# A mixture-of-experts decoder step: longer weight runs in ten slots, rows gathered two experts ahead

## Chip, cores, metric

The kernel runs on one core of a Trainium2 chip, with no other core at work. The metric is the device time of one execution in microseconds (us). "Span" is the time from the first to the last instruction in the profile of one execution.

## The reference, cut to what matters

One layer of a decoder runs on 280 tokens (16 meta tokens, 256 prompt tokens, 8 sample tokens) of width 2048, all in float32. An input projection feeds two recurrent branches, an output projection and a residual add give `x1`, and then comes the part that the change is about:

```python
xs = rmsnorm(x1, norm_ffn)                   # 280 x 2048
grp = top-1 of 4 expert groups               # softmax of xs @ w_coarse + b_coarse
e0, e1 = top-2 of the 8 experts in grp       # softmax of xs @ w_fine + b_fine
for e in 32 experts:                         # only the rows routed to e count
    act = silu(xs @ w_gate[e]) * (xs @ w_up[e]) * gate[:, e]   # 2048 x 512 each
    out += act @ w_down[e]                                      # 512 x 2048
y = rmsnorm(x1 + out, norm_final)
```

Each expert has 3 x 2048 x 512 float32 weights, 12.58 MB; the 32 experts have 403 MB, and all of it is read once.

## The kernel before, in words

**Stages.** After loads and norms come the input projection with the S5 scan, the HGRN2 heads, the output projection (L1174 to L1195, 8 blocks of 2.1 MB of `w_out` through ring slots 0 to 3), routing (L1198 to L1213 and L1650 to L1734), then the expert loop (`round_loads`, `round_act`, `round_rows`, `round_pe`, `round_dve`, one per engine, 32 experts in 16 double steps, b = 0 and 1), and a tail that adds each token's two expert rows to `x1`, normalises and stores. Every engine's stream is written out by hand and ordered by semaphores. A second round of the expert loop exists for experts with over 64 rows.

**Weights.** The ring has six slots of 2.1 MB: slots 2, 3, 0, 1 for an expert's gate and up weights, first half of the 2048 input rows and then the second, and 4, 5 for the two halves of its down weights. SyncE issues the loads in that order (L384, L390); gate and up of expert x+1 wait until TensorE has used that half of expert x, and down likewise. So the ring holds one expert. A load's rows are dealt `(k p) n`: partition p gets row k*128 + p for each k, in runs of one row: 2 KB for gate and up (8 runs a partition), 8 KB for down (2 runs).

**Rows.** `x1` goes to a DRAM tensor `x1_dram` (L499). For each expert VectorE makes a one-hot placing (L1740), TensorE turns it into a list of up to 64 tokens in bank 7 (`list_of`, L1221), VectorE reads indices and scales out of it (L1745 to L1750), and GpSimd gathers the 64 rows by an indirect DMA (L822) into one of two buffers, on partitions 0 to 63. TensorE transposes them in 16 steps (`turn_64`, L1228), with the rows as the stationary operand, 128 adjacent columns each; VectorE scales them by `norm_ffn` on the way out (L1755). The rows of expert x+1 are listed and gathered while TensorE is in gate and up of expert x.

**An expert on TensorE (L1244 to L1285).** List for x+1, 64 matmuls for gate and up (L1261), 16 transposes of the next rows, a wait for SiLU (L726), up (L727) and their product (L1780), 4 transposes of the product, a copy (L1785), and 32 matmuls with the down weights (L1282). ScalarE copies the result out (L732), GpSimd scatters it into `y_dram` (L839), waits for that to land and only then comes to its next gather.

Of the kernel before, what the change touches and what calls it, by code (L numbers as in the profile page):

```python
# [32 lines left out]
ALU = mybir.AluOpType  # L33
# [31 lines left out]
def hymba_step(nc, t):  # L65
# [27 lines left out]
    with ctx:  # L93
# [15 lines left out]
        vecs = sb("vecs", [P, 80])  # L109
        sc5 = sb("sc5", [P, 6, NJ])  # L110
# [104 lines left out]
        oh = Carver(arena, xnT_at)(3, CAP)  # L215
        c = Carver(arena, tab_at)
        lgT = Carver(arena, tab_at)(T)
        _, xg0, xg1 = c(D), c(D), c(D)
        xg = [xg0, xg1]
        yout = [c(D), c(D)]  # L220
        assert c.at <= AR_N
        c = Carver(arena, 0)
# [9 lines left out]
        gfin = Carver(arena, xnT_at + 3 * CAP)(D)  # L232
        ynorm = Carver(arena, tab_at)(D)
        V_COLS = D - 640

        route = sb("route", [P, 707])
# [5 lines left out]
        rankm = c(3, NE + 1)  # L242
        PL = c(3, NE + 1, 4)
        maxn, ext, mvals = c(1), c(ROUNDS - 1), c(33)
        assert c.at <= 707
# [4 lines left out]
        idx_dst = [sb(f"idx_dst{i}", [CAP, 1], U32) for i in range(2)]  # L250
        gcol = [sb(f"gcol{i}", [CAP, 1]) for i in range(2)]
# [12 lines left out]
        def sems(names):  # L264
# [3 lines left out]
        vec_loaded, s5_loaded, bc_loaded, wr_loaded = sems("vec_loaded s5_loaded bc_loaded wr_loaded")  # L268
        slot_loaded = [sem(f"slot_loaded{i}") for i in range(6)]
# [33 lines left out]
            "moe_done gfin_loaded ysum_done f_rms out_ready out_stored")  # L303
        yrow_loaded = [sem(f"yrow_loaded{i}") for i in range(3)]
# [16 lines left out]
        FILLS = [len(range(s, NPRE, PRE_SLOTS)) for s in range(4)] + [0, 0]  # L321
        MOE_SLOT = (2, 3, 0, 1)
# [36 lines left out]
        def slot(s, k):  # L359
            return ring[:, s, :].rearrange("p (k n) -> p k n", k=k)  # L360

        def run_rounds(eng, one_round):

            one_round(0)
            eng.wait_ge(lists_ready, 1)
            extra = eng.value_load(extra_i[0:1, 0:1], min_val=0, max_val=ROUNDS - 1)
            with eng.If(extra > 0):
                with eng.Fori(0, extra) as r:
                    one_round(r + 1)

# [8 lines left out]
        def _(sp):  # L379
            def load_gate_up(e, q):  # L380
                w = t["w_gate"] if q % 2 == 0 else t["w_up"]
                half = D // 2
                src = w[0][bass.ds(e, 1), (q // 2) * half:(q // 2 + 1) * half, :]
                sp.dma_start(slot(MOE_SLOT[q], KD // 2), src.rearrange("a (k p) n -> p (a k) n", p=P)) \  # L384
                    .then_inc(slot_loaded[MOE_SLOT[q]], 16)

            def load_down(e, s):
                half = FH // 2
                src = t["w_down"][0][bass.ds(e, 1), (s - 4) * half:(s - 3) * half, :]
                sp.dma_start(slot(s, KF // 2), src.rearrange("a (k p) n -> p (a k) n", p=P)) \  # L390
                    .then_inc(slot_loaded[s], 16)
# [24 lines left out]
            def load_vectors():  # L416
                for name, at in (("norm_mix", V_MIX), ("norm_ffn", V_FFN), ("s5_D", V_D), ("s5_b_glu", V_BGLU),
                                 ("s5_out_gain", V_G5), ("hg_lb_logits", V_LB0), ("hg_out_gain", V_GH)):
                    rows = t[name].rearrange("a (k p) -> (a k) p", p=P)
                    sp.dma_start(vrow[at:at + rows.shape[0], :], rows).then_inc(vec_loaded, 16)  # L420

# [53 lines left out]
            for n in range(OUT_AT + 2, NPRE):  # L475
                pre_load(n)
            for b in range(2):
                sp.wait_ge(S0_stored[b], 16 * len(range(b, NS, 3)))
# [6 lines left out]
            def round_loads(R):  # L485
                with sp.Fori(1 if is_first(R) else 0, NE) as e:
                    x = e + R * NE
                    for q in range(4):

                        sp.wait_ge(gate_up_done, x * 2 + (q // 2 - 1))  # L490
                        load_gate_up(e, q)
                    for s in (4, 5):
                        sp.wait_ge(down_done, x * 2 + (s - 5))
                        load_down(e, s)
# [6 lines left out]
            sp.wait_ge(logit_done, 1)  # L501
            sp.dma_start(gfin, t["norm_final"].rearrange("(a n) -> a n", a=1).broadcast_to([P, D])).then_inc(gfin_loaded, 16)

            run_rounds(sp, round_loads)
# [8 lines left out]
            for i, tile in enumerate(TILE_ORDER):  # L513
# [3 lines left out]
                if tile == 0:  # L517
                    sp.dma_start(y[0:P - NM, :], x1[NM:P, 0, :]).then_inc(out_stored, 16)
                elif tile == 1:
                    sp.dma_start(y[P - NM:2 * P - NM, :], x1[:, 1, :]).then_inc(out_stored, 16)  # L520
                else:
                    sp.dma_start(y[2 * P - NM:SEQ, :], x1[0:LAST, 2, :]).then_inc(out_stored, 16)
                    sp.dma_start(t["y_sample"][:, 0, :], x1[LAST:LAST + NS, 2, :]).then_inc(out_stored, 16)
# [9 lines left out]
        def _(act):  # L533
# [162 lines left out]
            act.wait_ge(S0_stored[2], 16 * len(range(2, NS, 3)))  # L696
            for o in range(NO):
                step.settle()
                for tile in range(3):
                    n = TT[tile]  # L700
                    act.wait_ge(x1_ready, 2 * o + 1 + tile // 2)
                    ins = nc.scalar.activation(yout[0][0:n, tile * CB:(tile + 1) * CB], x1[0:n, tile, o * CB:(o + 1) * CB], ACT.Square,
# [15 lines left out]
            def round_act(R):  # L718
                with act.Fori(0, NE // 2) as i:
                    for b in range(2):  # L720
# [10 lines left out]
                        for cc in range(4):  # L731
                            ins = nc.scalar.activation(yout[b][0:CAP, cc * 512:(cc + 1) * 512],  # L732
# [4 lines left out]
            for i, tile in enumerate(TILE_ORDER):  # L737
# [4 lines left out]
                step.link(nc.scalar.activation(ynorm[0:n, :], x1[0:n, tile, :], ACT.Square, accum_out=s))  # L742
# [5 lines left out]
        def _(pool):  # L748
# [67 lines left out]
            def gather(g, p):  # L816
# [5 lines left out]
                pool.indirect_dma_start(out=xg[p][0:CAP, :], out_offset=None, in_=x1_dram,  # L822
# [3 lines left out]
            def round_rows(R):  # L826
                if not is_first(R):
                    pool.wait_ge(tr_done, R * (NE + 1) + 1)
                gather(R * (NE + 1), 0)
                with pool.Fori(0, NE // 2) as i:  # L830
                    for b in range(2):
                        x = i * 2 + (R * NE + b)
                        g = i * 2 + (R * (NE + 1) + b + 1)

                        pool.wait_ge(tr_done, g)
                        gather(g, 1 - b)
# [3 lines left out]
                                                in_=yout[b][0:CAP, :], in_offset=None, bounds_check=last_row,  # L840
                                                oob_is_err=False).then_inc(scattered[b], 16)
                        pool.wait_ge(scattered[b], i * 16 + (R * (NE // 2) + 1) * 16)
                        pool.sem_inc(rows_free, 1)

# [5 lines left out]
            def add_rows(tile):  # L850
                n = TT[tile]
                pool.wait_ge(yrow_loaded[tile], 32)
                xt = x1[0:n, tile, cols]
# [3 lines left out]
            def norm_rows(i, tile):  # L857
# [3 lines left out]
                xt = x1[0:n, tile, cols]  # L861
# [15 lines left out]
        def _(pe):  # L877
# [347 lines left out]
            def turn_64(out, rows, waits):  # L1225

                eye = ident[0:CAP, 0:CAP]
                return pe.matmul(out, rows, eye, start=True, stop=True) if waits else pe.transpose(out, rows, eye)  # L1228

            def transpose_rows(p):  # L1230
                for k in range(KD):
                    ins = turn_64(PB[4 + k // 8][:, (k % 8) * CAP:(k % 8 + 1) * CAP], xg[p][0:CAP, k * P:(k + 1) * P], k == 0)
                ins.then_inc(tr_done, 1)

            def round_pe(R):
# [3 lines left out]
                else:  # L1239
                    pe.wait_ge(dst_ready, R * (NE + 1))  # L1240
                    pe.wait_ge(xgT_ready, R * (NE + 1))
                list_of(R * (NE + 1), 0)
                pe.wait_ge(gathered[0], R * (16 * 17) + 16)
                transpose_rows(0)  # L1244
                with pe.Fori(0, NE // 2) as i:
                    for b in range(2):
# [3 lines left out]
                        pe.wait_ge(dst_ready, g)  # L1250
                        list_of(g, i * 2 + (b + 1))

                        pe.wait_ge(xgT_ready, g)
                        for half in range(2):
                            sg_, su_ = MOE_SLOT[2 * half], MOE_SLOT[2 * half + 1]
                            pe.wait_ge(slot_loaded[sg_], x * 16 + 16 * (FILLS[sg_] + 1))
                            pe.wait_ge(slot_loaded[su_], x * 16 + 16 * (FILLS[su_] + 1))
# [591 lines left out]
```

## Time and profile before

| | |
|---|---|
| median of 3 runs | 1838.98 us (1836.88 to 1843.45) |
| the profiled execution | 1840.96 us, span 1838.9 us |
| granted TensorE clock, mean | 0.912 |
| bytes moved by DMA | 505.27 MB |
| output projection | 548 to 690 us |
| routing | 690 to 716 us |
| expert loop | 716 to 1790 us |
| tail | 1790 to 1839 us |

Loop and tail start and end where TensorE's first gate matmul starts and its last down matmul ends. DMA rates in GB/s are of the 16 queue engines together. A "share" of the DMA over 1 means that packets overlap on an engine.

### The profile page before, as it was taken

What the parts mean: (1) busy time and instruction counts of PE and PEld (TensorE: products, weight loads), DVE (VectorE), ACT (ScalarE), POOL (GpSimd) and SP (SyncE); (2) the same over time, 40 slices, a digit from 0 to 9 for tenths busy, and PEclk for the clock granted to TensorE, in tenths of its full rate; (3) what the DMA queues carried; (4) which work ended last, traced back from release to release, by engine and by line L of the source; (5) the groups of instructions that cost most, each with busy time, mean ns of one, the idle gap of its engine ahead of it and who ended that gap; (6) DMA issues with size and microseconds to landing.
All of it is one profiled execution on the core that took longest, in us unless ns stands there. A gap on an engine that the chain in (4) does not pass through costs nothing.

```text
span 1838.9 us, 19426 instructions
## 1 busy us (share of the span) xinstructions
PE 1486.7 (81%) x7565; PEld 839.3 (46%) x7565; DVE 566.0 (31%) x1407; ACT 285.2 (16%) x565; POOL 296.1 (16%) x402
## 2 busy tenths in 40 slices
PE   6899999798989996878787788788787787777870
PEld 5677776577758773433233233233233232233330
DVE  2779999666651223101010010010010010010015
ACT  2111111333320001111111011011011011011111
POOL 0066665333200000000000000000000000000006
PEclk9899999999979997988988998888999998899895
DMA  9324242335317625999999999999999999999964
GB/s 284 117 92 138 92 138 92 116 118 163 108 29 230 229 92 193 395 398 393 378 382 369 377 384 387 381 376 372 383 370 373 380 378 376 372 387 390 367 241 151
DMA packets 253055, 505.27 MB, mean 275 GB/s; under 512 B 23572, under 2 KB 99556, under 8 KB 233708
## 3 DMA queue, kind: packets, MB, share of 16 engines
q1 hardware_dynamic: 235788, 493.74, 74.5%
q0 software_dynamic: 5200, 9.19, 1.6%
q10 hardware_dynamic: 12016, 1.66, 0.6%
q8 instruction: 32, 0.52, 0.1%
q14 instruction: 19, 0.16, 0.0%
HBM read 503.18 MB, written 26.28 MB: 288 GB/s over the span
## 4 chain that ended last, share of the span: by engine, by line
DMA 35%; PE 26%; SPq 6%; DVE 1%; POOL 1%; issue 1%; ACT 0%; POOLq 0%; ACTq 0%; DVEq 0%
DMA ring<-in_w_up_dram 34%; PE bank L1261 16%; SPq L384 6%; PE bank L1191 6%; PE bank L1282 1%; PE bank L900 1%; DMA ring<-expert_rows 0%; PE bank L1158 0%; PE bank L1141 0%; POOL arena L862 0%; POOL arena L863 0%; PE bank L1169 0%; DVE arena L1798 0%; PE bank L1211 0%; PE bank L1228 0%
## 5 line engine op out<-in xcount | busy, mean ns | idle before, releaser
L1261 PE MATMUL bank<-ring,arena 128*64 128x512 f32 x2048 | 518.8, 664 | 156.8 <-DMA ring<-in_w_up_dram 156.8
L1261 PEld LDWEIGHTS bank<-ring,arena 128*64 128x64 f32 x2048 | 196.4, 152 | 452.6 <-issue 452.6
L1282 PE MATMUL bank<-ring,arena 128*64 128x512 f32 x1024 | 259.8, 666 | 19.0 <-DVE arena L1785 19.0
L1780 DVE SCALAR_TENSOR_TENSOR arena<-arena,gcol 64x512 f32<-64x512 f32 x32 | 23.8, 743 | 728.8 <-ACT arena L727 728.8
L930 PE MATMUL bank<-arena,ring 128*128 128x280 f32 x768 | 188.8, 405 | 3.0 <-ACT arena L579 1.9
L930 PEld LDWEIGHTS bank<-arena,ring 128*128 128x128 f32 x768 | 145.9, 192 | 44.1 <-issue 7.6
L1282 PEld LDWEIGHTS bank<-ring,arena 128*64 128x64 f32 x1024 | 80.5, 152 | 174.6 <-issue 174.6
L839 POOL DMA_INDIRECT expert_rows<-arena,idx_dst x32 | 29.5, 922 | 800.2 <-ACT arena L732 800.2
L732 ACT ACTIVATE arena<-bank 64x512 f32<-64x512 f32 x128 | 75.9, 593 | 330.0 <-PE bank L1282 328.8
L1191 PE MATMUL bank<-ring,arena 128*128 128x256 f32 x512 | 114.8, 386 | 0.0
L1228 PE MATMUL bank<-ident,arena 64*128 64x64 f32 x721 | 66.3, 239 | 56.7 <-DVE arena L1780 47.5
L1191 PEld LDWEIGHTS bank<-ring,arena 128*128 128x128 f32 x512 | 98.2, 193 | 17.1 <-issue 3.7
L822 POOL DMA_INDIRECT arena<-x_rows,idx_tok x33 | 31.0, 939 | 447.1 <-DVE gcol L1747 229.4
L1228 PEld LDWEIGHTS bank<-ident,arena 64*128 64x128 f32 x721 | 57.3, 155 | 87.2 <-DVE arena L1780 51.8
L1011 PE MATMUL bank<-arena,ring 128*128 128x280 f32 x256 | 74.4, 417 | 0.0
L1745 DVE TENSOR_SCALAR idx_tok<-bank 64x1 uint32<-64x1 f32 x33 | 5.0, 150 | 223.5 <-PE bank L1221 223.5
L726 ACT ACT_TABLE_LOAD x16 | 20.5, 1283 | 337.1 <-PE bank L1261 337.1
L726 ACT ACTIVATE arena<-bank,rcol 64x512 f32<-64x512 f32 x32 | 21.8, 683 | 289.6 <-PE bank L1261 289.4
L1495 DVE TENSOR_TENSOR_SCAN arena<-sc,arena 128x272 f32<-128x272 f32 x64 | 60.4, 983 | 1.1
L922 PE MATMUL bank<-ring,arena 128*128 128x256 f32 x256 | 59.5, 390 | 0.0
L922 PEld LDWEIGHTS bank<-ring,arena 128*128 128x128 f32 x256 | 49.1, 195 | 10.2 <-issue 3.6
L782 POOL TENSOR_TENSOR arena<-arena 128x272 f32<-128x272 f32 x32 | 21.8, 682 | 173.8 <-PE bank L987 91.3
(333 smaller groups left out, 1403.9 us busy)
## 6 DMA issues: line engine op xcount, KB each, us to landing
ring<-in_w_down_dram SPq DMA_DIRECT2D x64, 2048.0 KB, 21.2
ring<-in_w_gate_dram SPq DMA_DIRECT2D x64, 2048.0 KB, 19.6
ring<-in_w_up_dram SPq DMA_DIRECT2D x64, 2048.0 KB, 22.6
ring<-in_w_in_dram SPq DMA_DIRECT2D x20, 2048.0 KB, 8.7
ring<-in_w_out_dram SPq DMA_DIRECT2D x8, 2048.0 KB, 9.7
ring<-in_s_w_glu_dram SPq DMA_DIRECT2D x2, 2048.0 KB, 8.4
arena<-v_samples SPq DMA_DIRECT2D x8, 512.0 KB, 4.4
ring<-expert_rows SPq DMA_DIRECT2D x4, 1024.0 KB, 9.3
```

The source lines that it names most:

```text
L384: sp.dma_start(slot(MOE_SLOT[q], KD // 2), src.rearrange("a (k p) n -> p (a k) n", p=P)) \
L726: nc.scalar.activation(sg[0:CAP, :], PB[b][0:CAP, :], ACT.Silu, scale=rcol[b][:, 0:1])
L732: ins = nc.scalar.activation(yout[b][0:CAP, cc * 512:(cc + 1) * 512], PB[2 + cc // 2][(cc % 2) * CAP:(cc % 2 + 1) * CAP, :], ACT.Copy)
L822: pool.indirect_dma_start(out=xg[p][0:CAP, :], out_offset=None, in_=x1_dram, in_offset=bass.IndirectOffsetOnAxis(ap=idx_tok[p][:, 0:1], ax ...
L922: ins = pe.matmul(bank[:, tile * CB:(tile + 1) * CB], xnT[:, k, tile * P:(tile + 1) * P], w[:, k, :], start=(k == 0), stop=(k == KD - 1))
L930: ins = pe.matmul(bank[:, 0:T], w[:, k, b * P:(b + 1) * P], xnT[:, k, :], start=(k == 0), stop=(k == KD - 1))
L1011: ins = pe.matmul(PB[2][:, 0:T], slot(s, KD)[:, k, (i % 2) * P:(i % 2 + 1) * P], xnT[:, k, :], start=(k == 0), stop=(k == KD - 1))
L1191: ins = pe.matmul(PB[unit % 4][:, tile * CB:(tile + 1) * CB], yT[k][:, tile * P:(tile + 1) * P], slot(s, KD)[:, k, :], start=(k == 0), sto ...
L1228: return pe.matmul(out, rows, eye, start=True, stop=True) if waits else pe.transpose(out, rows, eye)
L1261: ins = pe.matmul(PB[b][at:at + CAP, :], xgT[b][:, kk, :], slot(s, KD // 2)[:, k, :], start=(kk == 0), stop=(kk == KD - 1))
L1282: ins = pe.matmul(PB[2 + cc // 2][at:at + CAP, :], hT[:, f, :], slot(4 + half, KF // 2)[:, k, cc * 512:(cc + 1) * 512], start=(f == 0), st ...
L1495: step.add(nc.vector.tensor_tensor_scan(M2[:, z], sc5[:, 0, j:j + 1].broadcast_to([P, TP]), M1[:, z], 0.0, ALU.mult, ALU.add))
```

## The change

Weights: all expert loads are dealt `(p k) n`, so that a partition gets one piece of DRAM of 16 KB (8 rows of gate or up, 2 rows of down). To match, the transposes take columns 8 apart (rows) and 2 apart (product), and a copy of `norm_ffn` in that order is loaded. There are ten slots: the six of the ring, two where the tables of the scan were, and two over `x1` itself. Gate and up have two sets of four slots, one for even and one for odd experts; down has ring slots 2 and 3. `x1` is read back from DRAM into two of the slots at the end. Rows: the list and the gather of expert x+2 are made in expert x; the two row buffers, and the two output buffers, are now the lower and upper 64 partitions of one tensor each. Some scratch moves (ScalarE's squares go to bank 7).

```diff
+        c = Carver(arena, x1_at)
+        x1_slots = [c(SLOT), c(SLOT)]
+        oh = c(3, CAP)
+        yout_both = c(D)
...
         c = Carver(arena, tab_at)
+        tab_slots = [c(SLOT), c(SLOT)]
+        xg_both = c(D)
...
+        x1_end, gfin = c(3, D), c(D)
...
+        halves = [slice(0, CAP), slice(CAP, P)]
+        xg, yout = ([buf[rows, :] for rows in halves] for buf in (xg_both, yout_both))
...
-        MOE_SLOT = (2, 3, 0, 1)
+        slots = [ring[:, i, :] for i in range(6)] + tab_slots + x1_slots
+        GATE_UP = ((6, 7, 4, 5), (0, 1, 8, 9))
+        DOWN = (2, 3)
...
-                sp.dma_start(slot(MOE_SLOT[q], KD // 2), src.rearrange("a (k p) n -> p (a k) n", p=P)) \
+                sp.dma_start(slot(s, KD // 2), src.rearrange("a (p k) n -> p (a k) n", p=P)) \
...
-            for n in range(OUT_AT + 2, NPRE):
+            for n in range(OUT_AT + 2, OUT_AT + 4):
                 pre_load(n)
+            sp.wait_ge(os_done, NS)
...
-            for s in (4, 5):
-                load_down(0, s)
             for q in range(4):
-                sp.wait_ge(out_done, 2 * (NO - 3 + q))
-                load_gate_up(0, q)
+                load_gate_up(0, 0, q)
+            for n in range(OUT_AT + 4, NPRE):
+                pre_load(n)
+            for h in range(2):
+                sp.wait_ge(out_done, 2 * (NO - 3 + h))
+                load_down(0, h)
+            sp.wait_ge(out_done, 2 * (NO - 1))
+            load_gate_up(1, 1, 0)
             sp.wait_ge(x1_ready, 2 * NO)
             for tile in range(3):
                 sp.dma_start(x1_dram[tile * P:tile * P + TT[tile], :], x1[0:TT[tile], tile, :]).then_inc(x1_stored, 16)
+            load_gate_up(1, 1, 1)
+            sp.wait_ge(x1_stored, 48)
             sp.wait_ge(logit_done, 1)
+            for q in (2, 3):
+                load_gate_up(1, 1, q)
+            def round_loads(R):
+                def down(x, e):
+                    for h in range(2):
+                        sp.wait_ge(down_done, x * 2 + (h - 1))
+                        load_down(e, h)
+                if is_first(R):
+                    down(1, 1)
+                with sp.Fori(1 if is_first(R) else 0, NE // 2) as i:
+                    for b in range(2):
+                        x = i * 2 + (R * NE + b)
+                        for q in range(4):
+                            sp.wait_ge(gate_up_done, x * 2 + (q // 2 - 3))
+                            load_gate_up(i * 2 + b, b, q)
+                        down(x, i * 2 + b)
...
+            sp.wait_ge(gate_up_done, extra * (2 * NE) + (2 * NE - 2))
+            for tile in TILE_ORDER:
+                sp.dma_start(x1_end[0:TT[tile], tile, :], x1_dram[tile * P:tile * P + TT[tile], :]).then_inc(x1_back[tile], 16)
...
-                        pool.wait_ge(tr_done, g)
-                        gather(g, 1 - b)
+                        pool.wait_ge(tr_done, i * 2 + (R * (NE + 1) + b + 2))
+                        gather(i * 2 + (R * (NE + AHEAD) + b + AHEAD), b)
                         pool.wait_ge(rows_ready, x + 2)
...
-                    ins = turn_64(PB[4 + k // 8][:, (k % 8) * CAP:(k % 8 + 1) * CAP], xg[p][0:CAP, k * P:(k + 1) * P], k == 0)
+                    half, kk = divmod(k, KD // 2)
+                    rows = xg[p][:, half * (D // 2):(half + 1) * (D // 2)].rearrange("t (p k) -> t k p", k=KD // 2)[:, kk, :]
+                    ins = turn_64(PB[4 + half][:, kk * CAP:(kk + 1) * CAP], rows, k == 0, p)
...
                         dve.wait_ge(act_ready, x + 1)
                         STT(hh[0:CAP, :], sg[0:CAP, :], gcol[b][:, 0:1], up[0:CAP, :], ALU.mult, ALU.mult).then_inc(h_made, 1)
+                        dve.wait_ge(h_made, x + 2)
+                        indices(g + 1, b)
                         dve.wait_ge(rows_free, x + 2)
-                        destinations(1 - b)
+                        destinations(g, 1 - b)
```

## Rows read from the trace of the kernel before

**Rows 1.** The page: the large DMA queue, and the chain by engine

```profile
q1 hardware_dynamic: 235788, 493.74, 74.5%
...
DMA 35%; PE 26%; SPq 6%; DVE 1%; POOL 1%; issue 1%; ACT 0%; POOLq 0%; ACTq 0%; DVEq 0%
```

**Rows 2.** Busy by stretch: length, engines, clock, DMA share, GB/s

```profile
780.00:1760.00 980.00, 764.34 (x3570) 308.56 (x3570) 86.38 (x261) 123.39 (x187) 52.91 (x57) 0.90 1.03 380
...
724.00:745.00 21.00, 18.15 (x91) 8.01 (x88) 2.70 (x6) 2.56 (x3) 0.00 (x0) 0.92 0.93 331
...
705.00:712.00 7.00, 1.54 (x11) 1.48 (x12) 1.12 (x8) 0.00 (x0) 1.12 (x1) 0.50 0.01 2
```

**Rows 3.** Chain of waits in the expert loop: start, us, what

```profile
759.60 3.04 SPq L384
...
960.25 3.47 SPq L384
963.82 20.28 DMA ring<-in_w_up_dram
...
984.24 9.69 PE bank L1261 x32
994.08 4.62 SPq L384
```

**Rows 4.** DMA packets of two stretches: 928 to 935 us, 949 to 953 us

```profile
DMA packets 1341, 2.71 MB, mean 387 GB/s; under 512 B 17, under 2 KB 17, under 8 KB 1341
...
DMA packets 232, 1.73 MB, mean 432 GB/s; under 512 B 10, under 2 KB 10, under 8 KB 25
```

**Rows 5.** Three whole stretches of down loads, by stretch as in rows 2

```profile
978.00:987.00 9.00, 4.81 (x18) 1.54 (x16) 0.00 (x0) 0.00 (x0) 0.93 (x1) 0.76 1.03 411
1013.00:1022.00 9.00, 4.64 (x20) 1.62 (x18) 0.00 (x0) 0.00 (x0) 0.94 (x1) 0.90 1.02 423
1047.00:1058.00 11.00, 6.08 (x22) 2.02 (x20) 0.00 (x0) 0.00 (x0) 0.93 (x1) 0.84 1.02 392
```

**Rows 6.** Timeline of TensorE over one expert: start, us, instructions, [idle before]

```profile
993.85 1.37 PE L1228 MATMUL bank<-ident,arena 64*128 64x64 f32 x17
997.43 0.62 PE L1228 MATMUL bank<-ident,arena 64*128 64x64 f32 x5 [2.21 <-DVE arena L1780]
998.64 8.78 PE L1282 MATMUL bank<-ring,arena 128*64 128x512 f32 x32 [0.59 <-DVE arena L1785]
1007.25 0.46 PE L1221 MATMUL bank<-route,arena 128*64 x6
1008.30 7.09 PE L1261 MATMUL bank<-ring,arena 128*64 128x512 f32 x32 [0.59 <-DMA ring<-in_w_up_dram]
1019.74 8.78 PE L1261 MATMUL bank<-ring,arena 128*64 128x512 f32 x32 [4.36 <-DMA ring<-in_w_up_dram]
```

**Rows 7.** SyncE's queue about the start of the loop

```profile
688.39 0.37 SPq L384 DMA_DIRECT2D ring<-in_w_up_dram  x1
690.19 1.35 SPq L499 DMA_DIRECT2D x_rows<-arena  x3
...
725.12 0.40 SPq L384 DMA_DIRECT2D ring<-in_w_gate_dram  x1
...
741.95 3.81 SPq L390 DMA_DIRECT2D ring<-in_w_down_dram  x2
```

**Rows 8.** Chain of waits, first and last expert

```profile
708.01 3.18 DMA arena<-x_rows,idx_tok
...
715.96 15.86 PE bank L1261 x63
...
1783.26 7.11 PE bank L1282 x32
```

**Rows 9.** The tile x_rows: who waited for the gathers; landing

```profile
  PEld bank L1228: 14.3, 7
...
DMA to landing us min/median/max: 3.2/7.5/9.0
```

**Rows 10.** Line L1228, 780 to 1760 us: duration in ns, min/median/max

```profile
L1228 PEld LDWEIGHTS bank<-ident,arena x638: 137/140/333, 791.8 to 1749.6; 64*128 64x128 f32 x160
```

More of the change, by code:

```diff
@@ L250, in hymba_step @@
         idx_dst = [sb(f"idx_dst{i}", [CAP, 1], U32) for i in range(2)]
+        dcol = [sb(f"dcol{i}", [CAP, 1]) for i in range(2)]
         gcol = [sb(f"gcol{i}", [CAP, 1]) for i in range(2)]
@@ L267, in hymba_step @@
         x_loaded = [sem(f"x_loaded{i}") for i in range(3)]
-        vec_loaded, s5_loaded, bc_loaded, wr_loaded = sems("vec_loaded s5_loaded bc_loaded wr_loaded")
-        slot_loaded = [sem(f"slot_loaded{i}") for i in range(6)]
+        vec_loaded, s5_loaded, bc_loaded, wr_loaded, gain_loaded = sems("vec_loaded s5_loaded bc_loaded wr_loaded gain_loaded")
+        slot_loaded = [sem(f"slot_loaded{i}") for i in range(10)]
         pool_consts, dve_consts, act_step, dve_step, pool_step = sems("pool_consts dve_consts act_step dve_step pool_step")
@@ L303, in hymba_step @@
             "moe_done gfin_loaded ysum_done f_rms out_ready out_stored")
+        x1_back = [sem(f"x1_back{i}") for i in range(3)]
         yrow_loaded = [sem(f"yrow_loaded{i}") for i in range(3)]
@@ L319, in hymba_step @@
         NPRE = OUT_AT + NO
-        FILLS = [len(range(s, NPRE, PRE_SLOTS)) for s in range(4)] + [0, 0]
-        MOE_SLOT = (2, 3, 0, 1)
+        FILLS = [len(range(s, NPRE, PRE_SLOTS)) for s in range(4)] + [0] * 6
+        slots = [ring[:, i, :] for i in range(6)] + tab_slots + x1_slots
+        GATE_UP = ((6, 7, 4, 5), (0, 1, 8, 9))
+        DOWN = (2, 3)
         EIGHTHS = 8
@@ L359, in slot @@
         def slot(s, k):
-            return ring[:, s, :].rearrange("p (k n) -> p k n", k=k)
+            return slots[s].rearrange("p (k n) -> p k n", k=k)
         def run_rounds(eng, one_round):
@@ L420, in load_vectors @@
                     sp.dma_start(vrow[at:at + rows.shape[0], :], rows).then_inc(vec_loaded, 16)
+                sp.dma_start(ffn_gain[:, :, :], t["norm_ffn"][0].rearrange("(h p k) -> p h k", h=2, p=P)).then_inc(gain_loaded, 16)
             for tile in TILE_ORDER:
@@ L474, in _ @@
             sp.dma_start(wr[:, :, NG:NG + NE], t["w_fine"][0].rearrange("(k p) n -> p k n", p=P)).then_inc(wr_loaded, 16)
-            for n in range(OUT_AT + 2, NPRE):
+            for n in range(OUT_AT + 2, OUT_AT + 4):
                 pre_load(n)
+            sp.wait_ge(os_done, NS)
+            for b in range(3):
+                sp.wait_ge(S0_stored[b], 16 * len(range(b, NS, 3)))
             for b in range(2):
-                sp.wait_ge(S0_stored[b], 16 * len(range(b, NS, 3)))
-            for s in (4, 5):
-                load_down(0, s)
+                sp.wait_ge(st_stored[b], 16 * NH // 2)
             for q in range(4):
-                sp.wait_ge(out_done, 2 * (NO - 3 + q))
-                load_gate_up(0, q)
[L485 to L494, printed above, removed]
+                load_gate_up(0, 0, q)
[6 more added lines that the diff above has]
+            load_gate_up(1, 1, 0)
             sp.wait_ge(x1_ready, 2 * NO)
@@ L828, in round_rows @@
                     pool.wait_ge(tr_done, R * (NE + 1) + 1)
-                gather(R * (NE + 1), 0)
+                for p in range(AHEAD):
+                    gather(R * (NE + AHEAD) + p, p)
                 with pool.Fori(0, NE // 2) as i:
@@ L843, in round_rows @@
                         pool.sem_inc(rows_free, 1)
+                pool.wait_ge(gathered[1], R * (16 * 17) + 16 * 17)
             run_rounds(pool, round_rows)
@@ L1223, in list_of, with turn_64 @@
                 ins.then_inc(list_done, 1)
-            def turn_64(out, rows, waits):
-                eye = ident[0:CAP, 0:CAP]
+            def turn_64(out, rows, waits, half):
+                eye = ident[halves[half], halves[half]]
                 return pe.matmul(out, rows, eye, start=True, stop=True) if waits else pe.transpose(out, rows, eye)
@@ L1654, in _ @@
             dve.wait_ge(part_logits, 1)
-            dve.wait_ge(S0_stored[2], 16 * len(range(2, NS, 3)))
             step.link(nc.vector.tensor_copy(lgT[0:NL, :], PB[6][0:NL, 0:T]))
@@ L1767, in round_dve @@
                     dve.wait_ge(rows_free, R * NE + 2)
-                places(0)
-                indices(g0, 0)
-                destinations(0)
-                rows_in(g0, 0)
+                for p in range(AHEAD):
+                    if p or not is_first(R):
+                        dve.wait_ge(list_done, g0 + p)
+                    places(p)
+                    indices(g0 + p, p)
+                destinations(g0, 0)
+                rows_in(t0, 0)
                 with dve.Fori(0, NE // 2) as i:
```

118 lines of the change are left out of this document (66 added, 52 removed).

## The prediction

> **What bounds the kernel now.** I read the page first: one DMA queue moves 493.74 of 505.27 MB and the chain that ends last is 35% DMA [rows 1], so the loads of weights are where to look. Then the busy times by stretch: in the expert loop, 780 to 1760 us, the DMA share is 1.03 at 380 GB/s, while TensorE is busy for 764 of 980 us at a mean granted clock of 0.90, that is, part of the time at the lower of its two levels, 1.2 GHz [rows 2]. A full DMA does not yet say that its rate sets the time, so I read the chain of waits: it repeats one figure, a half of gate and up on TensorE, SyncE's issue, a load of up weights of 20 us, the next half [rows 3]. From 759.60 to 994.08 us there are seven such turns, **33.5 us an expert**. The 20 us are mostly queueing: at 384 GB/s they are 7.8 MB, of which the load itself has 2.1. Bytes agree: 12.58 MB of weights, and some 0.3 MB of gathered and scattered rows, in 33.5 us are 384 GB/s. So the loop is bound by the DMA's rate, and freeing slots earlier would not by itself make it shorter.
>
> Could the rate rise? The DMA table for two short stretches shows that it depends on the run. In 928 to 935 us only the 2 KB packets of gate and up run, 387 GB/s; in 949 to 953 us nearly all bytes are the 8 KB packets of down, 432 GB/s [rows 4].
>
> **Weights in long runs.** Undisturbed, an expert now takes 8.39 MB / 387 + 4.19 MB / 432 = 21.7 + 9.7 = 31.4 us; measured are 33.5, so 2.1 us go to interruptions, row traffic among them. With 16 KB runs no row shows the rate; the nearest is the 8 KB one. Undisturbed: 12.58 / 432 = 29.1 us, the lower bound. Whole stretches of down loads with the row traffic in them run at 411, 423 and 392 GB/s [rows 5], by length 407; all weights at that rate take 30.9 us, and the 0.3 MB of rows 0.7 more: 31.7 us, the upper bound, since it has the row traffic hit all the time as it hits the down stretch. I take **31.2**, nearer to the upper end because the row traffic stays. That is 2.3 us an expert less.
>
> A rule speaks against this. The Trainium skill, DMA: Bandwidth & Descriptors, Specifications, gives 512 B as the least transfer for line rate; by it, 2 KB runs would be at line rate and longer ones would bring nothing. Here 387 against 432 GB/s [rows 4] disagrees. By the rule the sum would be that of the second rival.
>
> **Slots and order at the start.** Now the ring holds expert 0 at the start and expert 1's first load goes out at 725.12, when half of expert 0 has been used [rows 7]; between 705 and 712 us the DMA is idle (share 0.01) [rows 2]. After: gate and up of expert 0 go out during the output projection. They queue ahead of the third pair of `w_out` blocks: 8.4 MB, some 22 us, against blocks that are used 17.5 us apart and loaded four ahead, so TensorE does not feel it. Then down 0, and the first gate load of expert 1 before `x1` is stored at 690.19 [rows 7]; the other three behind it. These 8.6 MB (2.3 of rows, 6.3 of weights) run from 690 to about 712 us, so the first gather, at 708, no longer meets an idle DMA. Its 3.2 us [rows 8] become at most the median under load, 7.5 [rows 9]: between 0 and 4.3 us later, I take 3, as the queue is nearly drained. The second gather, the list of expert 1 and its indices run during the first gather: nothing; without that cover about 2 us once.
>
> SyncE then stands at down 1, which waits for the first half of down 0, now at 741.95 [rows 7], so at 745; behind that wait everything is queued, gate and up of expert 2 too, whose slots are free: the DMA idles from about 712 to 745. So the 8.4 MB of new room bring little: the old kernel has loaded 21 x 331 = 7.0 MB for expert 1 by then [rows 2]. From there the queue never runs dry: gate and up of x go out when x-2 is done, and down of x when down of x-1 is: 7 us after that was loaded, while gate and up of x still load for 14. The end of loading is 745 + 10.4 (down 1) + 30 x 31.2 = **1691 us**. Gate and up of expert 31 are there 10.4 us earlier, 1681; its second half takes 8.78, product and transposes 4.79 (993.85 to 998.64) [rows 6], down 7.11 [rows 8]: 1702. In the old kernel the last down ends at 1783.26 + 7.11 = 1790.4 [rows 8]. Gain **88.7 us**.
>
> **TensorE as the next in line.** Its own work in an expert, without waits for weights, is 7.09 + 8.78 (gate, up) + 13.9 (from 993.85 to 1008.30, less 0.59 of waiting) = 29.8 us [rows 6], under 31.2. That is the cover for all that follows.
> - Transposes from strided columns: not in the trace. The 17 instructions take 1.37 us and TensorE then waits 2.21 [rows 6], so they may become 2.6 times as long at no cost; a stationary load takes 140 ns now [rows 10]. Lower bound no change; upper below.
> - VectorE: a fourth index operation and a copy of the destinations (0.15 us each at most) between product and hT, beside 0.62 us of transposes: 0, or 0.1 us an expert without cover.
> - Gathers two ahead: TensorE waited 14.3 us in all for them [rows 9], while the DMA went on. 0 now, as the DMA sets the end; up to 14 if TensorE did.
> - GpSimd: the gather of x+2 waits for indices made after the product of x, before its scatter has data. Nothing stands behind it that is late.
> - ScalarE's squares in PSUM with one more wait, the second copy of `norm_ffn`: off the path.
> - `x1` read back and the last gain, 3.3 MB, behind the last down load: 8 us, until 1699, before the tail wants them at about 1717. Cover: the last down and the scatter; without it 8 us.
>
> The tail is otherwise the same. Sum: span 1838.9 - 88.7 = 1750.2. The profiled execution has 2.1 us around its span and stands 2.0 over the median of the runs, so the prediction for a run is **1750 us**.
>
> **Rivals.**
> 1. *Disturbances go with the short packets.* Then 29.1 us an expert, and TensorE's 29.8 decide: 719 + 32 x 29.8 = 1673, time 1721. For: the down stretches dip less. Against: the row traffic is unchanged. 9%.
> 2. *Long runs buy nothing* (they are still cut at each row, or DRAM gives no more). 33.5 us stay, only the start gains: 745 + 11.2 + 30 x 33.5 = 1761, end of down 1771, time 1819. For: no row has a 16 KB packet. Against: the 432 GB/s [rows 4]. 10%.
> 3. *TensorE becomes the bound through the transposes.* At twice their length: 17 x 0.28 - 3.58 = 1.2 and 4 x 0.14 = 0.6 more, 31.6 us an expert, 719 + 32 x 31.6 = 1730, time 1779. 9%. The Trainium skill, SBUF — State Buffer, Specifications (TRN2), asks for two hits in each 16-byte line for full bandwidth; columns 8 apart have one. No row shows such a load; doubling would be this rival.
> 4. *Slower: the same loads three times as long.* 420 ns each: 17 x 0.42 - 3.58 = 3.6 and 4 x 0.28 = 1.1, 34.5 us an expert, 719 + 32 x 34.5 = 1823, time 1872. It decides from 33.5 us on (1790 = 719 + 32 x 33.5), that is from about 370 ns a transpose. Against: the moving side, 64 columns, is unchanged, and 2.2 us are free. 4%.
>
> **How the numbers follow.** The forecast has 68%. Its bounds, 29.1 to 31.7 us an expert and 0 to 4.3 at the start, give 1721 (where TensorE stops it) to 1766. The range takes in rivals 1 and 3 and leaves out 2 and 4: 1705 to 1790, the low end below 1721 because TensorE at its higher clock all through would need less than 29.8. Faster by over 0.3% (5.5 us, about what a measurement can tell): the forecast and rivals 1 to 3, 96%, less one for what was not foreseen, 0.95; slower 0.03 and the same 0.02 share rival 4, whose price passes through zero near 370 ns, and the unforeseen.
>
> **What would show it.** Right: packets of over 8 KB in place of the 2 KB ones, about 410 GB/s in the loop, 31 us from expert to expert, the chain still of loads, the transposes within 3.6 us, TensorE waiting a little for weights, an idle DMA at about 715 to 745. Wrong: 380 GB/s with long packets; or a DMA share well under 1 in the loop with TensorE busy throughout; or transposes that end after the product is made.

## The result, and the profile after

The changed kernel takes **1774.04 us** (median of 4 runs, 1771.44 to 1777.56) where the kernel before takes 1839.9 us beside it: a ratio of 0.9645, 95% interval 0.9632 to 0.9658. The forecast was 1750 us, the range 1705 to 1790; 66 us are gained, 89 were forecast. The profiled execution takes 1773.67 us with a span of 1771.7.

The page of the changed kernel: the large queue (packets, MB, share), the queue of gathers and scatters, the chain by engine.

```profile
q1 hardware_dynamic: 113504, 496.04, 71.8%
q0 software_dynamic: 5280, 9.19, 1.6%
...
DMA 32%; PE 29%; issue 2%; DVE 2%; POOL 2%; SPq 1%; ACT 1%; POOLq 0%; ACTq 0%; DVEq 0%
```

Nearly the same bytes go in half as many packets as in [rows 1]. DMA and TensorE now share the chain almost evenly.

In the changed kernel L1310 is gate and up, L1333 down, L1271 the transposes; L401 issues the loads of gate and up, L407 those of down. In other runs these numbers shift by some lines. PE is TensorE's matmuls, PEld its loads of stationary operands, SPq SyncE's queue.

Busy by stretch, columns as in [rows 2]: start and end, length, busy us of PE, PEld, VectorE, ScalarE and GpSimd (with instructions), TensorE's clock, DMA share, GB/s.

```profile
705.00:712.00 7.00, 4.34 (x21) 4.24 (x22) 4.85 (x29) 0.00 (x0) 0.00 (x0) 0.50 1.01 425
712.00:745.00 33.00, 22.85 (x120) 12.46 (x119) 4.23 (x21) 2.56 (x3) 2.24 (x3) 0.76 0.18 73
780.00:1690.00 910.00, 774.92 (x3566) 340.15 (x3563) 86.69 (x288) 124.97 (x189) 53.08 (x58) 0.91 1.00 409
...
934.00:956.00 22.00, 20.95 (x104) 10.18 (x103) 3.04 (x10) 3.65 (x6) 1.86 (x2) 0.93 1.01 428
956.00:962.00 6.00, 5.53 (x30) 2.10 (x26) 0.00 (x0) 0.70 (x2) 0.00 (x0) 0.96 1.02 300
1056.00:1062.00 6.00, 6.00 (x24) 1.79 (x22) 0.00 (x0) 0.00 (x0) 0.00 (x0) 0.76 0.71 213
```

The DMA, idle before between 705 and 712 us, is full there, and idle from 712 to 745 instead. In the loop it moves 409 GB/s, 380 before [rows 2]. Two kinds of dip pull the mean under the 428 of an undisturbed stretch: at 956 the share stays at 1.02 while the rate falls to 300 (the rows of the gather issued at 952.21 pass), and at 1056 the share itself falls to 0.71 (nothing is queued).

DMA packets from 946 to 955 us, where hardly any rows move:

```profile
DMA packets 268, 3.90 MB, mean 433 GB/s; under 512 B 30, under 2 KB 30, under 8 KB 30
```

Packets of 16 KB thus run at 433 GB/s, as the 8 KB ones of [rows 4] did at 432.

The chain of waits (start, us, what), to be held against [rows 3, 8].

```profile
713.74 6.03 DMA arena<-x_rows,idx_tok
...
724.75 15.41 PE bank L1310 x63
...
810.43 37.14 DMA ring<-in_w_up_dram
...
998.48 40.98 DMA ring<-in_w_up_dram
1039.60 9.89 PE bank L1310 x32
...
1054.62 9.22 PE bank L1333 x32
...
1066.23 37.03 DMA ring<-in_w_up_dram
...
1636.68 39.54 DMA ring<-in_w_up_dram
1676.36 8.80 PE bank L1310 x32
1690.04 8.78 PE bank L1333 x32
1699.05 13.84 PE bank L1310 x64
...
1716.53 7.11 PE bank L1333 x32
```

The first three experts are TensorE's alone (no load in the chain until 810.43), and in the fourth it waits 0.35 us for one. Then a load of up weights of some 40 us, a half of gate and up, a down, and the next load repeat every second expert. From 810.43 to 1636.68 there are 26 experts: **31.8 us an expert**, 33.5 before. The last 47 us are TensorE's again.

SyncE's queue, as in [rows 7]:

```profile
750.34 3.76 SPq L407 DMA_DIRECT2D ring<-in_w_down_dram  x2
...
1060.43 3.77 SPq L407 DMA_DIRECT2D ring<-in_w_down_dram  x2
1064.74 0.33 SPq L401 DMA_DIRECT2D arena<-in_w_gate_dram  x1
```

Both dips of the share end with a down load: SyncE had stood waiting for the down slot, with the gate load queued behind it.

TensorE's timeline (as [rows 6]), and line L1271 (as [rows 10]):

```profile
982.43 2.33 PE L1271 MATMUL bank<-ident,arena 64*128 64x64 f32 x17
986.01 0.78 PE L1271 MATMUL bank<-ident,arena 64*128 64x64 f32 x5 [1.26 <-DVE arena L1837]
```

```profile
L1271 PEld LDWEIGHTS bank<-ident,arena x638: 189/203/353, 794.2 to 1689.1; 64*128 64x128 f32 x160
```

A stationary load of strided columns takes 203 ns (140 before). The 17 transposes grow from 1.37 to 2.33 us, and TensorE still waits 1.26 us for the product.

### The profile page after: what moved, and what is told of

It reads as the page before. It is cut to its first block, busy times and chain, and to the rows that moved or that the text cites. A ratio compares the mean times of both kernels' runs of the same rounds, so it can differ in the third digit from the quotient of the medians.

```text
span 1771.7 us, 19520 instructions
## 1 busy us (share of the span) xinstructions
PE 1504.0 (85%) x7571; PEld 873.4 (49%) x7571; DVE 566.3 (32%) x1445; ACT 285.1 (16%) x565; POOL 297.8 (17%) x403
## 3 DMA queue, kind: packets, MB, share of 16 engines
q0 software_dynamic: 5280, 9.19, 1.6%
## 4 chain that ended last, share of the span: by engine, by line
DMA 32%; PE 29%; issue 2%; DVE 2%; POOL 2%; SPq 1%; ACT 1%; POOLq 0%; ACTq 0%; DVEq 0%
DMA ring<-in_w_up_dram 31%; PE bank L1310 10%; PE bank L1333 9%; PE bank L1234 6%; PE bank L1271 1%; SPq L401 1%; PE bank L943 1%; DVE arena L1837 1%; ACT arena L767 1%; ACT arena L768 1%; POOL arena L898 0%; PE bank L1201 0%; DVE arena L1844 0%; PE bank L1184 0%; POOL arena L897 0%
## 5 line engine op out<-in xcount | busy, mean ns | idle before, releaser
L1310 PE MATMUL bank<-arena 128*64 128x512 f32 x1024 | 246.2, 635 | 63.2 <-DMA arena<-in_w_up_dram 63.2
L1333 PE MATMUL bank<-ring,arena 128*64 128x512 f32 x1024 | 271.7, 691 | 19.2 <-DVE arena L1844 19.2
L1310 PE MATMUL bank<-ring,arena 128*64 128x512 f32 x1024 | 240.4, 621 | 35.6 <-DMA ring<-in_w_up_dram 35.5
L1310 PEld LDWEIGHTS bank<-arena 128*64 128x64 f32 x1024 | 93.1, 146 | 202.7 <-issue 202.7
L1310 PEld LDWEIGHTS bank<-ring,arena 128*64 128x64 f32 x1024 | 98.0, 143 | 163.8 <-issue 163.8
L1333 PEld LDWEIGHTS bank<-ring,arena 128*64 128x64 f32 x1024 | 82.9, 158 | 184.6 <-issue 184.6
L773 ACT ACTIVATE arena<-bank 64x512 f32<-64x512 f32 x128 | 75.8, 592 | 346.7 <-PE bank L1333 345.6
L1271 PE MATMUL bank<-ident,arena 64*128 64x64 f32 x721 | 103.2, 292 | 26.0 <-DVE arena L1837 20.2
L1271 PEld LDWEIGHTS bank<-ident,arena 64*128 64x128 f32 x721 | 94.1, 225 | 56.1 <-issue 26.0
L880 POOL DMA_INDIRECT expert_rows<-arena,idx_dst x32 | 29.5, 920 | 355.7 <-ACT arena L773 355.7
```

Of the source, the lines that this page charges most:

```text
L773: ins = nc.scalar.activation(yout[b][:, cc * 512:(cc + 1) * 512], PB[2 + cc // 2][(cc % 2) * CAP:(cc % 2 + 1) * CAP, :], ACT.Copy)
L1310: ins = pe.matmul(PB[b][at:at + CAP, :], xgT[b][:, kk, :], slot(s, KD // 2)[:, k, :], start=(kk == 0), stop=(kk == KD - 1))
L1333: ins = pe.matmul(PB[2 + cc // 2][at:at + CAP, :], hT[:, f, :], slot(DOWN[half], KF // 2)[:, k, cc * 512:(cc + 1) * 512], start=(f == 0), ...
```

## The experiments

Ratios are to the kernel before, run beside each kernel. Diffs are against the changed kernel unless said otherwise.

**Each part alone.** *Short runs in the new kernel:*

```diff
...
-src.rearrange("a (p k) n -> p (a k) n", p=P)
+src.rearrange("a (k p) n -> p (a k) n", p=P)
...
-rows = xg[p][:, half * (D // 2):(half + 1) * (D // 2)].rearrange("t (p k) -> t k p", k=KD // 2)[:, kk, :]
+rows = xg[p][:, k * P:(k + 1) * P]
...
```

> The new kernel with its weights dealt as in the old one (2 KB runs for gate and up, 8 KB for down) and adjacent columns in the transposes; ten slots, order and early gathers stay. Theory (the gain is the packets' time): an expert goes back from 31.8 to about 33.5 us, 30 x 1.7 = 51 us, so about 1825 us, 380 GB/s in the loop. Rival (the gain comes from slots, order and gathers): 1774 us as the new kernel.

1837.98 us, 0.9982 (0.9968 to 0.9997). Slots and early gathers alone bring almost nothing, and the time is 13 us above what was expected. The loop (columns as in [rows 2]):

```profile
780.00:1680.00 900.00, 704.45 (x3297) 282.81 (x3292) 80.67 (x268) 113.86 (x172) 48.82 (x54) 0.89 1.03 381
```

A full DMA at 381 GB/s, the 380 of [rows 2].

*Long runs in the old kernel*, a diff against the kernel before (with the strided transposes and a gain in their order):

```diff
...
-src.rearrange("a (k p) n -> p (a k) n", p=P)
+src.rearrange("a (p k) n -> p (a k) n", p=P)
...
```

> The old kernel (six slots, gather one ahead) with 16 KB runs and the columns that go with them, and nothing else. Theory: most of the gain, 31.5 to 31.8 us an expert instead of 33.5, about 1785 us. Rival (long runs need the slots, since with six the queue runs dry once packets are faster): 1810 us or more, with a DMA share under 0.97 in the loop.

1833.68 us, 0.9954 (0.9936 to 0.9971). The part that the forecast gave most of the gain to brings 8 us of 66 by itself. Its loop, and its chain:

```profile
780.00:1680.00 900.00, 713.07 (x3310) 352.04 (x3307) 78.52 (x239) 116.29 (x176) 50.17 (x54) 0.84 0.95 382
```

```profile
1016.76 6.41 DMA expert_rows<-arena,idx_dst
...
1024.12 9.38 DMA arena<-x_rows,idx_tok
...
1050.53 7.11 DMA expert_rows<-arena,idx_dst
```

The DMA is no longer full (0.95) and no load of weights is in the chain. A scatter that lands, then a gather that lands, then TensorE and the next scatter: 33.77 us a turn. The share under 0.97 is the sign that was named for the rival, too few slots; the run with six slots below shows that it is not they.

*Gathers one expert ahead in the new kernel* (the lists, gathers and indices of the kernel before):

```diff
...
-                        pool.wait_ge(tr_done, i * 2 + (R * (NE + 1) + b + 2))
-                        gather(i * 2 + (R * (NE + AHEAD) + b + AHEAD), b)
+                        pool.wait_ge(tr_done, g)
+                        gather(g, 1 - b)
...
```

> The new kernel with lists and gathers one expert ahead, as in the old kernel. Theory (gathers are hidden while the DMA sets the time): 1774 us, within 3 us. Rival (TensorE would wait for rows, since a gather now shares the engines with 16 KB packets and comes after the scatter has landed): up to 15 us more, 1790 us.

1862.32 us, 1.0105 (1.0073 to 1.0138): 88 us slower than the changed kernel, and far above both figures expected. The loop; who waited for the gathers, as in [rows 9] (us, times); the chain over one turn (L1270 is the transposes, L1832 the copy of the product, L1329 down, L773 the copy out):

```profile
780.00:1680.00 900.00, 690.94 (x3263) 339.17 (x3261) 77.74 (x237) 112.27 (x171) 48.30 (x52) 0.85 0.93 374
```

```profile
  PEld bank L1270: 262.3, 32
...
DMA to landing us min/median/max: 3.4/8.9/13.9
```

```profile
1030.73 8.02 DMA expert_rows<-arena,idx_dst
...
1039.70 8.98 DMA arena<-x_rows,idx_tok
...
1048.72 3.15 PE bank L1270 x22
1051.90 0.43 DVE arena L1832
...
1052.46 8.83 PE bank L1329 x32
...
1061.92 0.59 ACT arena L773
...
1064.53 8.49 DMA expert_rows<-arena,idx_dst
```

The **row loop** closes here: GpSimd waits until the scatter has landed, only then issues the next gather; TensorE waits for that, transposes, does the down matmuls, ScalarE copies out, the next scatter goes. 33.80 us a turn, and TensorE waits 262 us for gathers, 14.3 before [rows 9].

**The loop opened at another place.** Gathers still one ahead, but GpSimd issues the gather of x+1 before it waits for the scatter of x-1 to land (against the kernel just shown):

```diff
                         pool.wait_ge(tr_done, g)
                         gather(g, 1 - b)
+                        pool.wait_ge(scattered[1 - b], i * 16 + (R * (NE // 2) + b) * 16)
+                        pool.sem_inc(rows_free, 1)
                         pool.wait_ge(rows_ready, x + 2)
...
-                        pool.wait_ge(scattered[b], i * 16 + (R * (NE // 2) + 1) * 16)
-                        pool.sem_inc(rows_free, 1)
```

> The kernel with lists and gathers one expert ahead again (1862 us), but GpSimd now issues the gather of x+1 before it waits for the scatter of x-1 to land, instead of after. Theory (a closed loop sets the time there: scatter 8 us, gather 9, transposes 3, down 9, copy out 2.4, with 3 of issue and handing over, 34 us): without the scatter in it the loop is open, a gather fits beside the 14 us of gate and up, and the DMA sets the time again, about 1775 us. Rival (a gather one expert ahead is too late in itself, since its list is only made when gate and up begin): 1825 us or more, with TensorE still waiting for rows in each expert.

1782.91 us, 0.9684 (0.9658 to 0.9710): 79 of the 88 us are back. Its loop, the waits for gathers, a piece of the chain:

```profile
780.00:1680.00 900.00, 758.27 (x3518) 335.48 (x3514) 83.67 (x255) 122.20 (x186) 53.82 (x58) 0.91 0.99 404
```

```profile
  PEld bank L1278: 34.6, 15
```

```profile
1001.16 40.68 DMA ring<-in_w_up_dram
```

With the scatter's landing out of the loop the DMA is full and loads of weights are in the chain again. It was this closed loop, not the distance of the gathers as such; the distance is left with at most the other 9 us.

**Slots.** One set of four gate and up slots in place of two, so that gate and up of x+1 wait for x:

```diff
...
-        GATE_UP = ((6, 7, 4, 5), (0, 1, 8, 9))
+        GATE_UP = ((6, 7, 4, 5), (6, 7, 4, 5))
...
-sp.wait_ge(gate_up_done, x * 2 + (q // 2 - 3))
+sp.wait_ge(gate_up_done, x * 2 + (q // 2 - 1))
...
```

> The new kernel with one set of four slots for gate and up (with down, six slots as in the old kernel), gate and up of expert x+1 waiting for those of x; long runs and gathers two ahead stay. Theory (long runs need only the early gather, not the slots): an expert as in the new kernel, 31.8 us, and 7 to 10 us more at the start, about 1785 us. Rival (six slots cannot keep the queue filled): 1800 us or more, with a DMA share under 0.97.

1776.39 us, 0.9646 (0.9621 to 0.9672), the changed kernel's own ratio. The four added slots bring nothing that the medians can tell apart. In the profiled executions the stretch from the first scatter to the last is 6.5 us shorter with ten slots (969.9 and 976.4 us), but it begins 6.1 later (757.0 and 750.9): the first gather meets the early loads (6.03 us in place of 3.21), and the output projection began later (553.70 and 548.96). So the parts stand thus (us):

| | gathers one ahead | gathers two ahead |
|---|---|---|
| short runs | 1839.9 (six slots, before) | 1837.98 (ten) |
| long runs | 1833.68 (six), 1862.32 (ten) | 1776.39 (six), 1774.04 (ten) |

**SyncE's order.** Gate and up of x+2 ahead of down of x+1, so that the start is not held by the wait for the down slot:

```diff
...
+                with sp.Fori(0, NE // 2 - 1) as i:
+                    x = i * 2 + R * NE
+                    gate_up(x + 2, i * 2 + 2, 0)
+                    down(x + 1, i * 2 + 1)
+                    gate_up(x + 3, i * 2 + 3, 1)
+                    down(x + 2, i * 2 + 2)
...
```

> The new kernel with SyncE's order turned: gate and up of expert x+2 are issued ahead of down of x+1, so they no longer stand behind the wait for down of x. Theory (the wait at down holds the queue: the DMA idles from 712 to 745 us, and again for some us in some experts): loading starts again about 10 to 15 us earlier and the dry stretches in the loop go, about 1755 us. Rival (the DMA is full in the loop and the start is hidden): 1770 us or more. Other rival: down now comes late, behind 8.4 MB, and TensorE waits for it: over 1774 us.

1769.13 us, 0.9604 (0.9575 to 0.9633): about 5 us, at the edge of what the intervals tell apart. The stretch at the start, a group of TensorE's waits from 780 to 1680 us (us in total, times, longest; L1342 is down) and a piece of the chain:

```profile
712.00:745.00 33.00, 24.70 (x117) 11.88 (x119) 4.59 (x13) 2.56 (x3) 1.48 (x2) 0.76 0.48 194
```

```profile
PEld bank L1342 <- DMA ring<-in_w_down_dram: 151.9, 53, 4.8
```

```profile
826.71 27.02 DMA ring<-in_w_down_dram
```

In these 33 us 194 - 73 = 121 GB/s more are moved, 4.0 MB or some 10 us of the loop; but now down comes late, and TensorE waits for it: from the first scatter to the last the profiled execution takes 970.4 us, the changed kernel's 969.9.

**What the rows cost.** Gathers and scatters stay, but move no expert's rows; the tail reads `x1` in place of the scattered ones:

```diff
-last_token, last_row = pool.to_reg(T - 1), pool.to_reg(2 * T - 1)
+last_token, last_row = pool.to_reg(0), pool.to_reg(0)
...
-sp.dma_start(yrow[2 * tile + j][0:TT[tile], :], y_dram[r0:r0 + TT[tile], :])
+sp.dma_start(yrow[2 * tile + j][0:TT[tile], :], x1_dram[tile * P:tile * P + TT[tile], :])
```

> The new kernel with the bound of gather and scatter set to 0, so that only rows of index 0 move, and the tail adds rows of x1 instead of the experts' rows: the routed rows are left out, every instruction is still issued. Theory (row traffic is what keeps an expert at 31.8 us): 29.3 to 30 us, with TensorE's own 29.8 next, about 1715 us. Rival (the loss is elsewhere, in the issue order or in DRAM): 1765 us or more.

1705.6 us, 0.9252 (0.9227 to 0.9278), 68 us under the changed kernel. The loop:

```profile
780.00:1640.00 860.00, 773.70 (x3633) 348.98 (x3631) 88.06 (x290) 125.34 (x190) 54.77 (x59) 0.92 1.01 427
```

At 427 GB/s an expert's 12.58 MB take 29.5 us. The rows' 9.19 MB would take 22 us at that rate; they cost three times as much.

*The gather's rows alone left out* (`last_row` and the tail as they were):

> The new kernel with the bound of the gather set to 0, so that only row 0 of x1 moves; the scatter is left as it is. The gathered rows are left out. Without both, 1706 us were measured, 68 less. Theory (both directions cost alike): about 1740 us. Rival 1 (the gather, which reads DRAM beside the weights, costs most): 1720 us or less. Rival 2 (the scatter, which writes DRAM, costs most): 1760 us or more.

1723.21 us, 0.9351 (0.9326 to 0.9375): 51 of the 68 us are the gather's; the other 17, by difference, are the scatter's, which was not left out alone.

*Rows spread over the 64 places.* An expert has few rows (280 x 2 / 32 = 17.5 on average), in the first places of its list. Place 4a+c is given row 16c+a:

```diff
-nc.vector.tensor_copy(slotid, iota_i[:, 0:CAP])
+nc.vector.tensor_copy(slotid.rearrange("p (a c) -> p a c", c=4), iota_i[:, 0:CAP].rearrange("p (c a) -> p a c", a=16))
```

> The new kernel with the rows of an expert dealt over its 64 places 4 apart (place 4a + c has row 16c + a) instead of into the first places. An expert has 17.5 rows on average. Theory (the gathered and scattered rows, always in the first places, all go through the same 5 or so of the 16 DMA engines, so that these engines carry 8 x 0.31 = 2.5 us of rows beside 29.3 us of weights, which makes the 31.8 us of an expert, while the others run dry): spread over 16 engines it is 0.7 us, 30.0 us an expert, about 1720 us, 425 GB/s in the loop. Rival (rows cost by what they do to DRAM or to a mixed queue, wherever they go): 1774 us.

1766.7 us, 0.9588 (0.9565 to 0.9611): 7 us, with the intervals apart; in the profiled executions the stretch from the first scatter to the last is 3.3 us shorter (966.6 and 969.9), and 3.0 were there at the first scatter. It is the lowest median of the versions that compute all of it, but the theory that the rows' cost comes from their lying on few engines expected 1720 us. It falls for most of the cost as far as the edit does spread the rows over more engines, which is not shown: no trace names the engine of a packet.

*The same in the kernel before:*

> The old kernel with the same dealing of rows and nothing else. Theory of the few engines: some 1.5 us of 33.5 an expert, about 1795 us. Rival: as the old kernel, 1840 us; also if TensorE's wait for the gather takes the place at once.

1837.03 us, 0.9980 (0.9964 to 0.9995): some 3 us.

*Both edits, the order and the spread:*

> Both changes that made the new kernel a little faster: gate and up of x+2 issued ahead of down of x+1, and rows dealt 4 places apart. Theory (one serves the start, the other the rows' time): the gains add, 5 + 8 us, about 1760 us. Rival (both remove the same dry stretches): as the better one alone, 1767 us.

1767.35 us, 0.9594 (0.9572 to 0.9615). The gains do not add.

**The transposes.** Adjacent columns for rows and product, and the old order of `norm_ffn`; the columns then don't meet the rows of the weights they belong to:

```diff
...
-rows = xg[p][:, half * (D // 2):(half + 1) * (D // 2)].rearrange("t (p k) -> t k p", k=KD // 2)[:, kk, :]
+rows = xg[p][:, k * P:(k + 1) * P]
...
```

> The new kernel with its transposes of rows and of the product reading adjacent columns as in the old kernel, and the old order of norm_ffn; the weights keep the new order, so the columns no longer meet their weights. A stationary load in the transposes takes 203 ns in the new kernel against 140 in the old. Theory (the 17 before the product are done while TensorE would wait for it, and the DMA sets the time): 1774 us, within 4. Rival (TensorE's own chain is as long as the DMA's): 20 x 0.06 us x 32 = 38 us less, about 1736 us.

1774.28 us, 0.9631 (0.9607 to 0.9656). A stationary load takes 140 ns again, and nothing is gained: here striding costs nothing on the path. With the closed loop, where the transposes are in the chain, it was not tried.

## Why the prediction was right, and where it was wrong

The direction, the range and most of the size held; what the gain was given to did not. That the total held was in part luck: by the forecast's own sum the kernel with its gathers one expert ahead would take the same 1750 us, 14 more at the most, and it takes 1862.32.

**The sum.** The last down was to end at 1702 and ends at 1716.53 + 7.11 = 1723.6, 21.6 us later. By the forecast's own order of loads, gate and up of expert 4 land at 745 + 10.4 + 2 x 31.2 + 20.8 = 838.6; they land at 810.43 + 37.14 = 847.6, 9.0 late. 5.3 of these were there at the start: SyncE's wait ended at 750.34, not 745. That is most likely no part of the change: the output projection starts at 553.70 in this execution and at 548 in the profiled one of before; in other executions of kernels that are the same up to there it starts between 549 and 554. The other 3.7, and 17.4 in the 26 experts from there to 1676.2, are the step from expert to expert, 31.8 or more in place of 31.2. From 1676.2 to the last down it takes 47.4 us where the forecast had 52, since TensorE does the last expert without a wait: 4.5 come back. 5.3 + 3.7 + 17.4 - 4.5 = 21.9, the 21.6 but for rounding. The tail is as before, 48 us. The remaining 2 of the 24 us between 1750 and 1774 are how execution and median stand: the forecast put the median 2.0 under the profiled execution, and here the two agree.

**"Weights in long runs"** was near in its rate: 31.8 against 31.2, a little over the upper bound of 31.7. The nearest row was the right price (433 against 432 GB/s), and what stayed is the row traffic. The 512 B rule of the Trainium skill, DMA: Bandwidth & Descriptors, Specifications, gives 512 B as enough for line rate and disagrees here too: the loop of the same kernel moves 381 GB/s with 2 KB runs for gate and up, 409 with the long ones.

**"Gathers two ahead … 0 now … up to 14 if TensorE did" is the step that failed.** Beside long runs the term was worth 88 us (1862.32 to 1774.04). It was priced by a wait, TensorE's 14.3 us [rows 9], and the wait was small because the weights were later still. What had to be summed was the loop that the gather is part of. The trace of before shows it. The tile of the scattered rows, kernel before, who waited for it and its landing; and GpSimd's issues over one turn:

```profile
  POOL arena L822: 217.7, 31
...
DMA to landing us min/median/max: 3.2/7.0/12.3
```

```profile
973.89 0.92 POOL L839 DMA_INDIRECT expert_rows<-arena,idx_dst  x1 [22.12 <-ACT arena L732]
982.00 0.93 POOL L822 DMA_INDIRECT arena<-x_rows,idx_tok  x1 [7.19 <-issue]
1010.69 0.92 POOL L839 DMA_INDIRECT expert_rows<-arena,idx_dst  x1 [27.76 <-ACT arena L732]
```

GpSimd waited 7.0 us in every expert for the scatter before it came to the gather. A turn without waits for weights or for the product can be estimated from this trace: 8.1 us from a scatter's issue to the next gather's (982.00 - 973.89), 7.5 for the gather [rows 9], 1.37 + 0.62 for the transposes and 0.59 for the copy of the product [rows 6], and 12.1 from the start of the down matmuls (998.64 [rows 6]) to the next scatter's issue. These are 30.2 us, only 1.0 under the forecast's time of a new expert; that the long runs would stretch the turn past it could not be read there. With the long runs the turn grows to 33.8: scatter and gather take 15.8 and 17.0 us together in the turns shown, 14.5 in the medians of before, and the strided transposes 3.15 in place of 1.99. The granted clock is lower too, 0.84 and 0.85 in these loops where it was 0.90 [rows 2]; an expert's down matmuls, which lie in the turn, are busy for 302.2 / 32 = 9.4 us in the run with long runs alone and for 259.8 / 32 = 8.1 in the kernel before (fifth part of the two pages). So the kernel before had **two loops**, 33.5 us of weights and, by this estimate, some 30 of rows, and long runs alone shorten the first but lengthen the second. The change shortened one and opened the other, and only the two together bring 66 us.

**"Slots and order at the start"** held: the DMA idles from 712 to 745 (share 0.18), and the new room brings little. The first gather took 6.03 us where 3.2 + 3 were forecast. "From there the queue never runs dry" was wrong in places, as at 1056 us; by the run with SyncE's order turned, mending that, the start included, is worth about 5 us, since down is late next.

**"TensorE as the next in line"** held for the transposes: 1.45 times as long a load, within the free 2.6. The other edits costed at nothing were not tried one by one; none of them shows in the chain above. The Trainium skill, SBUF — State Buffer, Specifications (TRN2), asks for two hits in each 16-byte line for full bandwidth. The trace agrees in sign, 203 ns with one hit and 140 with adjacent columns; the factor of two of rival 3 is 1.45 here.

**The rivals.** The 29.1 us of the first were not met: the dips stayed with the long packets, and even with no rows moved the loop needs 29.5. The second, that long runs buy nothing, came true only where the row loop was left closed, by a mechanism that it did not name. The third came close to the measured time with 1779, by a cause that is not there: with the columns adjacent the time is the same. The fourth fell with it.

**Open.** Why the rows cost three times their bytes; and why ten slots with the closed loop are 29 us slower than six. The spans of the two profiled executions differ by 1863.7 - 1833.8 = 29.9 us. Of these 6.3 are there at the first scatter (757.1 and 750.8 us). The rest is the turn: the single ones shown are equal (33.80 and 33.77), but from the first scatter to the last it takes 34.25 us on average with ten slots, (1818.9 - 757.1) / 31, and 33.49 with six, (1788.9 - 750.8) / 31. In the median the scatter lands after 8.1 us with ten slots and 6.7 with six, the gather after 8.9 and 9.4. The length of the runs does bear on the landings: with ten slots and gathers two ahead the medians are 6.8 and 6.9 us with short runs, 8.2 and 9.0 with long ones. What the slots do to them was not tried.

## What to carry to other kernels

A wait that looks small behind the bound is not the price of what causes it: follow the waiting work around until it comes back to itself, add up that loop from the same trace, and hold it against the bound's own time an iteration. Where two loops are nearly as long, shortening one alone hardly pays, and a run of one part alone tells nothing against it. Take the landing of a store out of such a loop first: issuing the next load ahead of that wait gave 79 of 88 us with no new buffer.

## What was not expected of the hardware

- Row traffic of 9.19 MB, 1.8% of the bytes, costs 68 us of 1774, three quarters of it for the gather. While rows pass, the rate falls from 428 to 300 GB/s at an unchanged share of 1.0: loads are queued, but the packets take longer. Whether all engines are held so, or some idle while packets overlap on others, the share does not tell.
- A packet of 16 KB brings no more than one of 8 KB (433 and 432 GB/s), while 2 KB to 8 KB brought 387 to 432.
- A stationary load of 128 columns that lie 8 apart takes 203 ns, of adjacent ones 140. Where the transposes are off the path this costs nothing (1774.28 and 1774.04 us).
